# The chunk loop of a gated delta rule: k k^T of chunks 2 to 7 loaded from DRAM instead of computed

## What is computed

```python
lower = jnp.where(strict, jnp.einsum('bhncd,bhnsd->bhncs', k_beta, k) * decay, 0.0)
sol = lax.linalg.triangular_solve(lower, rhs, left_side=True, lower=True, unit_diagonal=True)
...
def step(state, inp):
    u_i, w_i, q_i, k_i, a_i, cd_i = inp
    v_new = u_i - jnp.einsum('bhcd,bhde->bhce', w_i, state)
    o_i = jnp.einsum('bhcd,bhde->bhce', q_i, state) + jnp.einsum('bhcs,bhse->bhce', a_i, v_new)
    state = state * cd_i[..., None, None] + jnp.einsum('bhcd,bhce->bhde', k_i, v_new)
```

## Time and profile before

| | |
|---|---|
| median of 3 runs | 1340.1 us |
| the profiled execution | 1339.84 us |
| its span, first to last instruction | 1338.1 us |
| TensorE busy (matmuls) | 1269.7 us, 95% |
| mean granted TensorE clock | 0.979 of full speed |
| VectorE / ScalarE / GpSimd busy | 53% / 43% / 54% |
| chain of work that ended last | TensorE 63%, GpSimd 14%, issue 10%, VectorE 4%, ScalarE 4%, DMA 3% |

### The profile page before, as it was taken

The page is one execution under the profiler, slowest core; times in us unless marked ns, Lnnn a source line. Parts: engine busy times, 40 slices in busy tenths (PEclk is TensorE's granted clock), DMA queues, the critical chain, the costliest instruction groups (busy, mean ns, idle before and its releaser), DMA issues.

```text
span 1338.1 us, 16940 instructions
## 1 busy us (share of the span) xinstructions
PE 1269.7 (95%) x6138; PEld 1054.7 (79%) x6138; DVE 714.5 (53%) x860; ACT 581.2 (43%) x841; POOL 727.3 (54%) x484
## 2 busy tenths in 40 slices
PE   2799999999999999999699999999999999999997
PEld 2568888888888999787578888888888878888886
DVE  2834525254375555356655655665566556458445
ACT  3233615446456554616734434444444443215321
POOL 3455777668971534212766565656565676426440
PEclk8599999999999999999899999999999999999999
DMA  8242343414633303010122333233323258435501
GB/s 325 73 110 79 98 106 94 117 55 127 174 64 65 110 16 110 24 31 1 32 61 71 90 96 95 58 85 95 95 62 81 87 173 314 142 118 177 203 15 63
DMA packets 155499, 133.49 MB, mean 100 GB/s; under 512 B 16479, under 2 KB 131756, under 8 KB 155436
## 3 DMA queue, kind: packets, MB, share of 16 engines
q1 hardware_dynamic: 155436, 132.65, 33.1%
HBM read 114.50 MB, written 18.13 MB: 99 GB/s over the span
## 4 chain that ended last, share of the span: by engine, by line
PE 63%; POOL 14%; issue 10%; DVE 4%; ACT 4%; DMA 3%; SPq 1%; POOLq 0%; ACTq 0%; DVEq 0%
PE ps L2316 18%; PE ps L2317 18%; PE ps L2318 18%; POOL ada_raw L928 4%; POOL ada_raw L931 3%; POOL w_split L903 3%; PE ps L2510 2%; POOL ada_raw L933 2%; DMA ada_first<-in_ada_w_dram 1%; DVE ada_first L1716 1%; POOL h_p L1061 1%; POOL ada_sum L937 1%; PE ps L2529 1%; DMA x_hi<-in_x_dram 1%; PE ps L2526 1%
## 5 line engine op out<-in xcount | busy, mean ns | idle before, releaser
L2316 PE MATMUL ps<-h_p,w_units 128*128 128x512 f32 x616 | 242.0, 393 | 11.6 <-POOL h_p L1061 10.1
L2317 PE MATMUL ps<-h_p,w_units 128*128 128x512 f32 x616 | 241.3, 392 | 0.0
L2318 PE MATMUL ps<-h_p,w_units 128*128 128x512 f32 x616 | 241.2, 392 | 0.0
L2316 PE MATMUL ps<-h,w_split 128*128 128x512 f32 x448 | 176.0, 393 | 0.0
L1072 POOL TENSOR_TENSOR w_units<-f_units,w_units 128x512 fp32r<-128x512 f32 x88 | 112.9, 1294 | 114.7 <-ACT w_units L1531 47.6
L2318 PE MATMUL ps<-h,w_split 128*128 128x512 f32 x448 | 174.4, 389 | 0.0
L2317 PE MATMUL ps<-h,w_split 128*128 128x512 f32 x448 | 174.4, 389 | 0.0
L1097 POOL TENSOR_TENSOR wd_split<-wd_raw,wd_split 128x1024 fp32r<-128x1024 f32 x44 | 110.1, 2508 | 109.6 <-ACT wd_split L1627 109.5
L2316 PEld LDWEIGHTS ps<-h_p,w_units 128*128 128x128 f32 x616 | 116.7, 190 | 37.3 <-issue 8.4
L2267 DVE TENSOR_TENSOR ad_split<-ad_raw,ad_split 128x512 fp32r<-128x512 f32 x40 | 98.8, 2484 | 78.0 <-ACT ad_split L1628 78.0
L2316 PE MATMUL ps<-wd_split,ad_split 128*128 128x512 f32 x352 | 137.1, 390 | 2.1 <-DVE ps L2225 1.8
(11 more groups left out here) (338 smaller groups left out, 2384.8 us busy)
## 6 DMA issues: line engine op xcount, KB each, us to landing
w_up_raw<-in_w_up_dram SPq DMA_DIRECT2D x44, 512.0 KB, 5.3
wd_raw<-in_w_down_dram SPq DMA_DIRECT2D x44, 512.0 KB, 4.2
ada_raw<-in_ada_w_dram SPq DMA_DIRECT2D x32, 512.0 KB, 4.2
w_raw<-in_w_in_dram SPq DMA_DIRECT2D x28, 512.0 KB, 5.2
act_dram<-cg SPq DMA_DIRECT2D x22, 512.0 KB, 3.3
ad_raw<-act_dram SPq DMA_DIRECT2D x44, 256.0 KB, 4.5
ada_first<-in_ada_w_dram SPq DMA_DIRECT2D x4, 2048.0 KB, 17.4
h_room<-in_w_out_dram SPq DMA_DIRECT2D x8, 512.0 KB, 8.0
```

What stands on the lines that cost most here:

```text
L2316: pe.matmul(dst, a_hi, b_hi, start=(first and n == 0), stop=False, skip_group_check=onto)
L2317: pe.matmul(dst, a_hi, b_lo, start=False, stop=False, skip_group_check=onto)
L2318: mm = pe.matmul(dst, a_lo, b_hi, start=False, stop=(last and n == len(pairs) - 1), skip_group_check=onto)
```

## The change

`load_chunk_kk(n)` on SyncE reads k k^T of chunk n, for 4 heads, from `kk_dram` into the columns of `k_t` that chunk n - 2 held, 128 partitions x 4 pieces of 512 bytes, 256 KB. `chunk_product` of chunks 2 to 7 takes its first operand from there, not from PSUM bank 1, and waits on `kk_early`, not on `dn_kk`. `key_products(n)` leaves TensorE's loop; it stays in `opening()` for chunks 0 and 1. The load of `x2` over `k_t` gets one wait more.

```diff
+        E_KK_LEFT = 16 * NH
...
+            def load_chunk_kk(n):
+
+                sp.wait_ge(s.dn_kc, n - 1)
+                sp.dma_start(k_t[:, :, (n - 2) * P:(n - 1) * P],
+                             kk_dram[:, n, 0:P * P].rearrange("h (r c) -> r h c", c=P)).then_inc(s.kk_early, 16)
...
+            load_chunk_kk(2)
             load_gates(2)
+            load_chunk_kk(3)
             sp.wait_ge(s.ada_mm, NH)
...
             for n in range(4, TT):
+                load_chunk_kk(n)
                 load_gates(n)
+            sp.wait_ge(s.dn_a, (TT - 1) * A_STEPS + A_LT0)
             for tt in range(0, TT, 2):
...
             def chunk_product(n, slot):
 
                 dve.wait_ge(s.dn_a, n * A_STEPS + A_MASK)
-                dve.wait_ge(s.dn_kk, n + 1)
-                dve.tensor_tensor(lt[:, slot, :, :], bank(1, 1, P), dec[:, :, :], ALU.mult).then_inc(s.dn_a, 1)
+                if isinstance(n, int) and n < 2:
+                    dve.wait_ge(s.dn_kk, n + 1)
+                    product = bank(1, 1, P)
+                else:
+                    dve.wait_ge(s.kk_early, E_KK_LEFT + 16 * (n - 1))
+                    product = k_t[:, :, ds((n - 2) * P, P)]
+                dve.tensor_tensor(lt[:, slot, :, :], product, dec[:, :, :], ALU.mult).then_inc(s.dn_a, 1)
...
                 if b:
                     level_b(n - 1, 1 - slot, 0, "T")
-                if a:
-                    key_products(n)
                 if b:
                     level_b(n - 1, 1 - slot, 1, "P")
```

## The result

The changed kernel takes 1345.47 us (median of 6 runs, 1344.35 to 1348.87) against 1340.2 us before (median of 6 runs); the ratio is 1.0046, with a 95% interval of 1.0035 to 1.0056. It is slower by 5.3 us by the medians (6.2 by the ratio), where I had forecast no difference and a range that ended at 1343.0. The profiled execution of after has a span of 1344.4 us against 1338.1.

The account below looks back on a forecast made before the run. In the loop's steps ScalarE's chain to rr was taken to cover the removed TensorE work. The sum was 1339.84 - 0 + 0 + 0 = 1339.8 us, forecast as 1340.0, with an 8-in-10 range of 1337.6 to 1343.0.

Parts of the forecast that it names:

- The chain: Chunk loop, step 3: from VectorE's um_done (446.69) over ScalarE alone to rr (452.02), then TensorE at 452.65; key_products not in it.
- part 1: Removing key_products from six loop steps: 5.4 us of TensorE at face value, 0 on the path, covered by ScalarE's chain to rr.
- the 0.14 for slower: Chance of the whole kernel being slower by over 0.2% (2.7 us), summed as 0.09 + 0.03 + 0.02.
- Part 2: VectorE's chunk_product operand from SBUF: bound 0 to 0.58 us a step, up to 3.5 us; taken as 0 on the path.
- Rival (c): chunk_product's two SBUF operands beside late GpSimd, VectorE's 1.22 us idle gone: 0.58 us a step, +3.5, 1343.3 us; chance 0.03.
- Part 3: Six matrix loads, 0.9 us each: w_out released some 1.8 us later, within 2.24 us of room; 0 on the path.
- Rival (b): w_out over 2.24 us late, GpSimd's qd delays decays(3): 0 to 3.9 us; chance of loss 0.25, over 2.7 us 0.09.
- Rival (a): TensorE bounds the loop, so removed products count: -5.4 us, 1334.4; milder, long steps only, -2.7, 1337.1; chance 0.06 together.

Follow-up runs that it names:

- r9_gap_split: Against the changed kernel, one wait more and no work more: TensorE starts level 1 P only after ScalarE has written egb of the same chunk; 1346.69 us, ratio 1.0036.

## Why the prediction was wrong

**What held.** The chain was read rightly: the removed products lie on the side where ScalarE is last, level 1 P in the short steps starts when `um` is there, the freed time goes into the wait for `rr`, and no step got shorter. The waits came out as forecast, 5.9 us for 5.7.

**The step that failed** is the last one of part 1: "On the path it is 0", with ScalarE's chain as the only cover named. It took idle time on TensorE as free; measured, the chunk loop got 7.3 us longer. The matmuls behind the wait were priced at the durations of before, and those were measured at the full clock, which the removed work helped to keep. I quoted the granted clock of 1.00 and asked how long TensorE would be idle (1.6 us, right), but never what the clock does then; no rival had it, and the 0.14 for slower was made of other things. The price can be bounded from rows: from the product with `rr` to `um_done` are 9.6 us (437.07 above to 446.69), nearly all of it matmuls, and from the start of that product to the next group are 1.87 us at the lower clock (436.61 to 438.48) against 1.00 at the upper (456.50 to 457.50). So, as an estimate, a fall that lasted through the whole path would cost some 8 us, three times; the first of the three lasted for about 9 us and cost 4.3, the others lasted 3 and cost 1.4 and 1.5. The trace of before also shows where such a fall happens, in a stretch of the same kernel in which TensorE waits for the norm:

```profile
644.00:654.00 10.00, 5.26 (x27) 4.01 (x25) 8.59 (x22) 7.83 (x17) 5.78 (x5) 0.87 0.39 105
654.00:664.00 10.00, 8.47 (x32) 6.55 (x32) 5.00 (x10) 5.69 (x12) 9.72 (x9) 0.79 0.00 1
```

The Trainium skill bears on this: "TensorE: Matmul & The Clock Gate", section "Part 1: The HAM clock gate (the "warmup" mystery)", says that TensorE's clock has a half-rate and a full-rate state, that the half rate is the default, and that activity lifts it. The trace agrees with the two states (PEclk 0.50 and 1.00 above).

**Part 2** (the operand, 0 us) was right. `chunk_product` of after takes what it took before:

```profile
L1838 DVE TENSOR_TENSOR lt<-k_t,dec x6: 681/682/683, 437.3 to 525.1; 128x512 f32<-128x512 f32 x6
```

The row gives nanoseconds, least, median and most. Rival (c) fell with it and with the products put back. Its condition never held: GpSimd ran nothing beside any of the six, so what two operands in SBUF cost beside GpSimd was not tested here. In before the mask L1815 shows that cost: 1.26 us beside GpSimd, 0.69 with GpSimd idle:

```profile
452.14 0.69 DVE L1815 TENSOR_TENSOR dec<-dec,causal 128x512 f32<-128x512 f32 x1 [1.01 <-ACT dec L1227]
```

**Part 3** (the loads, 0 us) was right in its sum and too dear in its term: w_out was to land 1.8 us later, and GpSimd's work on it began at 440.83 instead of 440.29, 0.54 us later; counted from the issue of the first DMA of the group (425.11 in after, 425.56 before) it is 1.0 us. In all eleven profiles it starts 14.5 to 14.8 us behind that first issue without the loads (three kernels) and 15.3 to 16.3 with them (eight).

```profile
440.83 4.65 POOL L1047 TENSOR_TENSOR h_room<-h_room,gate_row 128x1024 f32<-128x1024 f32 x2 [8.52 <-DMA h_room<-in_w_out_dram]
```

The six matrix loads took 3.1 to 8.0 us to land, and VectorE waited for none. Rival (b) has the sign that came out and not the cause: the kernel without any load was as slow. Rival (a), a gain, fell in this order of work, and came true, at 3.0 of its 5.4 us, in the order that makes TensorE the bound.

## What to carry to other kernels

Work on TensorE that hides behind another engine may still be worth something: before it is taken out, add the new idle time to the waits near it, look at the granted clock row by row, and price the matmuls that come next at half speed as well. If a wait is going to grow, put later work that has its inputs into it; here 1.33 us a step, moved ahead of the wait, turned a loss of 5.3 us into a gain of 7.5. Two executions of a kernel near that edge can differ by several us, so one profile isn't enough to say on which side it is.

## What the runs showed that I had not expected

- Removing 0.9 us of matmuls three times made the chunk loop 7.3 us longer. In the changed kernel the granted clock fell within waits of 1.58 and 1.83 us, and matmuls ran at half speed for about 9 us behind the first and for about 3 us behind the others.
- The clock can fall while TensorE works: in r9_gap_split it fell at 435.4 us, in the last records of level 1 P, after a wait of 1.59 us in front of that group.
- The same wait has different outcomes: after 1.83 us the clock fell in one kernel's profile, after 1.84 it stayed in another's.
- Two loads of 256 KB in 512-byte pieces, the one in front of the gates and the other in front of w_out, moved w_out's landing by 0.4 to 1.7 us from the first issue, in most profiles by about 1.0, where their transfer time at 293 GB/s would give 1.8.
